# Gate and up products spread over eight PSUM banks, and the transposes of the attention output put on other banks and later, in a two-layer streaming encoder

## The reference, cut to what matters

```python
def ffn_half(x, g, w_gate, w_up, w_down):
    h = rms_norm(x, g)
    a = jax.nn.silu(jnp.einsum('bsd,df->bsf', h, w_gate)) * jnp.einsum('bsd,df->bsf', h, w_up)
    return x + 0.5 * jnp.einsum('bsf,fd->bsd', a, w_down)
...
for l in range(DEPTH):                       # 2 layers
    yp = ffn_half(yp, g_ffn1[l], ...)        # D_MODEL 1024, D_FF 2816
    qa, ka, va, qb, kb, vb = project(rms_norm(yp, g_mix[l]), w_in[l], ...)
    oa = band_attn_prompt(qa, ka, va, ...)   # group A: 8 heads of 64, own chunk of 64 rows and 8 before
    ob = diff_post(diff_attn_prompt(qb, kb, vb, lam), ...)  # group B: 4 heads, softmax 1 - lam * softmax 2
    yp = yp + out_proj(oa, ob, w_out[l])
    yp = ffn_half(yp, g_ffn2[l], ...)
    # the same for ys, the next 64 frames of running streams, against their caches
```

## Time and profile before

| | |
|---|---|
| runs of the kernel before | 8454.6, 8012.99 and 7601.93 us, median 8012.99 |
| profiled execution | 7586.13 us, span 7585.1 us on the slowest core |
| spans of the 8 cores | 7554.7 to 7585.1 us, mean granted clock 0.958 to 0.965 |
| busy: PE, DVE, ACT, POOL | 6630.0, 2912.0, 2651.3, 1403.3 us |
| moved | 1130.56 MB, 149 GB/s over the span |

### The profile page before, as it was taken

The page is one execution under the profiler, slowest core; times in us unless marked ns, Lnnn a source line. Parts: engine busy times, 40 slices in busy tenths (PEclk is TensorE's granted clock), DMA queues, the critical chain, the costliest instruction groups (busy, mean ns, idle before and its releaser), DMA issues.

```text
span 7585.1 us, 114887 instructions; the slowest of 8 cores (7554.7 to 7585.1 us)
## 1 busy us (share of the span) xinstructions
PE 6630.0 (87%) x39776; PEld 3525.2 (46%) x39776; DVE 2912.0 (38%) x5057; ACT 2651.3 (35%) x4204; POOL 1403.3 (19%) x1750
## 2 busy tenths in 40 slices
PE   5777788989899998989898989899999989896777
PEld 2333334454444445454444454544444454555666
DVE  4545534343333343333434343433343433433332
ACT  1412315151524335261414152524333351614343
POOL 1112111202111121212121212121121212122121
PEclk9899999999999999999999999999999999998888
DMA  8699762424233342424242424243343424256666
GB/s 264 216 310 306 224 206 85 146 86 157 97 121 122 115 154 69 147 73 160 97 146 98 158 89 142 95 148 116 109 134 103 148 70 149 77 181 213 208 222 200
DMA packets 452258, 1130.56 MB, mean 149 GB/s; under 512 B 38384, under 2 KB 166128, under 8 KB 451696
## 3 DMA queue, kind: packets, MB, share of 16 engines
q1 hardware_dynamic: 433568, 1059.23, 43.5%
q0 software_dynamic: 18128, 63.97, 2.2%
HBM read 973.12 MB, written 149.95 MB: 148 GB/s over the span
## 4 chain that ended last, share of the span: by engine, by line
PE 61%; DVE 11%; ACT 10%; issue 7%; DMA 5%; POOL 4%; SPq 2%; DVEq 0%; ACTq 0%; POOLq 0%
PE psb L542 14%; PE psb L522 12%; PE psb L518 11%; PE psb L756 5%; POOL tC L533 4%; PE psb L889 3%; PE psb L986 3%; PE psb L1007 3%; DVE tA L528 2%; PE psb L696 2%; ACT tA L531 2%; ACT eT L1065 2%; SPq L270 1%; PE psb L1166 1%; ACT tq L759 1%
## 5 line engine op out<-in xcount | busy, mean ns | idle before, releaser
L533 POOL TENSOR_TENSOR tC<-tA,rstdT 128x512 f32<-128x512 f32 (+1 forms) x792 | 954.4, 1205 | 4198.5 <-ACT tA L531 4081.0
L522 PE MATMUL psb<-hT,wring 128*128 128x512 bf16 (+1 forms) x6336 | 1430.9, 369 | 132.3 <-DVE BIG L536 126.6
L518 PE MATMUL psb<-hT,wring 128*128 128x512 bf16 (+1 forms) x6336 | 1434.5, 369 | 87.2 <-DVE tA L528 78.6
L542 PE MATMUL psb<-BIG,wring 128*128 128x512 bf16 (+1 forms) x6336 | 1322.5, 370 | 43.8 <-DVE wring L412 38.6
L531 ACT ACTIVATE tA<-tA 128x512 f32<-128x512 f32 (+1 forms) x792 | 479.8, 606 | 2218.3 <-DVE tA L528 2217.9
L536 DVE TENSOR_TENSOR BIG<-psb,tC 128x512 bf16<-128x512 f32 (+1 forms) x792 | 524.2, 662 | 1757.8 <-POOL tC L533 1757.8
L522 PEld LDWEIGHTS psb<-hT,wring 128*128 128x128 bf16 x6336 | 588.1, 98 | 895.0 <-issue 355.3
L518 PEld LDWEIGHTS psb<-hT,wring 128*128 128x128 bf16 x6336 | 618.9, 98 | 785.6 <-issue 133.4
L542 PEld LDWEIGHTS psb<-BIG,wring 128*128 128x128 bf16 x6336 | 621.1, 98 | 735.4 <-issue 76.9
L528 DVE TENSOR_TENSOR tA<-psb,rstdT 128x512 f32<-128x512 f32 (+1 forms) x792 | 515.7, 651 | 164.7 <-ACT rstdT L485 164.6
L994 ACT ACTIVATE eT<-psb 128x1024 bf16<-128x1024 f32 (+2 forms) x640 | 532.7, 892 | 106.4 <-PE psb L986 57.5
(11 more groups left out here) (179 smaller groups left out, 6233.0 us busy)
## 6 DMA issues: line engine op xcount, KB each, us to landing
wring<-wsc SPq DMA_DIRECT2D x1280, 512.0 KB, 3.9
wsc<-wring SPq DMA_DIRECT2D x160, 512.0 KB, 9.4
vb<-w_gate SPq DMA_DIRECT2D x66, 512.0 KB, 9.7
vb<-w_up SPq DMA_DIRECT2D x66, 512.0 KB, 10.7
vb<-w_down SPq DMA_DIRECT2D x66, 512.0 KB, 12.3
vb<-cbk SPq DMA_DIRECT2D x64, 512.0 KB, 5.1
vb<-cbv SPq DMA_DIRECT2D x64, 512.0 KB, 4.5
vb<-w_in SPq DMA_DIRECT2D x36, 512.0 KB, 11.6
```

Of the source, the lines that this page charges most:

```text
L518: P.add("pe", lambda kc=kc, bg=bg, wg=wg, fl=fl: nc.tensor.matmul(psb[bg][:, 0:T], wg[:, kc, fl * 128:(fl + 1) * 128], hT[:, kc, 0:T], sta ...
L522: P.add("pe", lambda kc=kc, bu=bu, wu=wu, fl=fl: nc.tensor.matmul(psb[bu][:, 0:T], wu[:, kc, fl * 128:(fl + 1) * 128], hT[:, kc, 0:T], sta ...
L533: P.add("pool", lambda ts=ts: nc.gpsimd.tensor_tensor(out=tC[ts][:, 0:T], in0=tA[ts][:, 0:T], in1=rstdT[:, 0:T], op=ALU.mult), [("t", ts, ...
L542: P.add("pe", lambda: nc.tensor.matmul(psb[ab][:, 0:T], wd[:, fl, dcl * 128:(dcl + 1) * 128], aT[:, fc, 0:T], start=(fc == 0), stop=(fc == ...
```

## The change

Three things are edited. In `ffn` the pair of banks is now `2 * (fc % 4)` and the next, so the pairs go round all eight banks and block fc has the pair of block fc - 4. `rot()` was called 44 times in a pass of `ffn`, a multiple of 4, so its state for the other users is as before. `o_transpose` takes its bank as an argument: in group B's part the transposes of a head come 4 tiles after its last one for i = 0 (2 before) and 6 for i = 1 (4 before), both in bank 4 now; for i = 2 and 3 they stay 6 tiles after it in bank 6. Those of the last head are moved from after unit 4 to after unit 6 of group A, in bank 7. In `a2` the call of `o_transpose(0, hp - 1)` now stands ahead of the norm of u = 3, not behind it.

```diff
             for fl in range(2):
                 fc = 2 * ft + fl
-                bg, bu = rot(), rot()
+                bg = 2 * (fc % 4)
+                bu = bg + 1
...
-        def o_transpose(half, hh):
-            bt = 6
+        def o_transpose(half, hh, bt):
             pv = psb[bt][:, 0:256].bitcast(BF16)
...
-                    deferred.append([idx + min(nk // 2, 6), o_transpose, (1, h)])
+                    lag = 4 if i == 0 else 6
+                    deferred.append([idx + lag, o_transpose, (1, h, 6 if lag <= nk // 2 else 4)])
...
+            if u == 3 and hp > 0:
+                o_transpose(0, hp - 1, 6)
             if u % 2 == 1:
                 ob4 = psb[ob][:, 0:260].rearrange("p (x f) -> p x f", x=4)
...
-            if u == 3 and hp > 0:
-                o_transpose(0, hp - 1)
...
-            if idx == 4:
-                flush(10 ** 9)
-        o_transpose(0, 3)
+            if idx == 6:
+                for d_ in deferred:
+                    d_[1](1, 3, 7)
+                deferred.clear()
+        o_transpose(0, 3, 6)
```

## The result

The changed kernel took 7842.65, 7508.26, 7720.16 and 7487.98 us, median **7614.21 us** (a fifth execution, not in the median, took 7481.87); the kernel before, with one run more than in front, has a median of 7807.46. In part of the executions of either kernel the cores of one die run at a lower granted clock and the time is some per cent longer, and the ratios here leave such executions out while the medians do not. The ratio is **0.9863, 95% interval 0.9817 to 0.9909**; measured again (r1_changed_again) it was 0.9878, 0.9852 to 0.9903. So the change makes the kernel 1.2 to 1.4% faster by these two measurements. The forecast was 7467 us in a range of 7415 to 7545, a ratio of 0.984.

A forecast was written before the change was run, and what follows sets the result against it. PE's work bounds the kernel, with some 955 us of standing; in gate and up the ring DVE, ACT, POOL, DVE sets the pace. 66.4 + 0 + 4.8 + 35 + 13 = 119 us off 7586.1 gives 7467 us, range 7415 to 7545.

The forecast's parts named there:

- the target and its range: Whole kernel: 7467 us, range 7415 to 7545, forecast given 0.62, for an execution like the profiled one.
- the sum: Whole kernel: gains of 66.4, 0, 4.8, 35 and 13 us, 119 us together, taken from 7586.1 us.
- within 2%: Whole kernel: a change too small to be told from no change, about 2%, given 0.77.
- Gate and up, 512 columns: 28 passes after the first group: eight banks move PE forward 11 matmuls, 2.37 us a pass, 66.4 us.
- the first rival: Gate and up products: the whole gap goes, 113 in place of 66.4 us, 7420 us in all; chance 0.12.
- First group: Its four passes: 0 gained, as down products await weight casts on DVE; at most 9.5 us.
- Last group: Its four passes of 256 columns: 11 matmuls of 0.109 us gained in each, 4.8 us.
- Group A: 16 attentions, transposes ahead of the norm: 0.95 us at two boundaries and 0.3 at the end, 35 us.
- Group B, i = 0: Attention, later transposes: a head takes 7.3 us in place of 8.36, 1.1 us gained 12 times, 13 us.
- The clock: The 28 passes: a granted clock of 0.92 would cost 287 us more, 7754 us in all; chance 0.04.
- the rival for a slower kernel: The 28 passes: new waits or denser work lower PE's clock, deciding from 0.965 on, 7754 us; chance 0.04.
- The five terms: Gate and up 66.4 us, first group 0, last group 4.8, group A's attention 35, group B's 13.

The follow-up runs named there:

- r1_changed_again: The changed kernel measured once more, nothing edited, against the kernel before: ratio 0.9878, 0.9852 to 0.9903; median over all its executions 7627.6 us.

## Why the prediction was right or wrong

**The step that failed is the target and its range.** The prediction said that the runs shown "have a median of 8012.99, but their fastest, 7601.93, is what the profiled execution answers to, and the prediction is for an execution of that kind". It thereby put at nothing the time that an execution loses when the cores of one die run at a lower granted clock, and built the range of 7415 to 7545 from costs of the change alone. The runs showed that loss in its place: 7720.16 and 7842.65 us, with the cores of one die at a mean clock of 0.905 and 0.882, beside 7487.98 us with all cores at 0.953 to 0.958. The median over the four executions, 7614.21, is the mean of 7508.26 and 7720.16. The three executions at 7481.87, 7487.98 and 7508.26 us lie inside the range, 15 to 41 us above the 7467. The warning was on record: two of the three runs shown lay 427 and 868 us above the profiled execution, with the same program, and each is more than every term of the sum. What makes a die run at the lower clock in one execution and not in the next is open. The ratio was right: 0.984 forecast, inside the first interval and 0.001 outside the second; so was "within 2%", to which the prediction gave 0.77.

**Gate and up, 512 columns: right, in size and in mechanism.** 66.4 us were forecast, 108.5 - 42.2 = 66.3 came on core 0, from stretches of 77.0 and 76.2 us and a new wait at the fourth down matmul. The 28 waits are 0.45 to 2.37 us and 36.8 us together, where 1.0 or 2.3 and some 46 were forecast: the forecast took 81.57 and 79.48 us for every stretch before, and the means of the 14 of each kind are 81.18 and 79.37. Six banks, the order of the first down matmuls and the opened ring each moved that wait as the mechanism says, and the first rival, the whole gap, is out. By its ratio the edit alone gave 57 us; the difference to 66 is within its interval (35 to 78).

**First group: right.** Its gate and up stretch stood still, 104.30 us, and its four stretches together (441.9 us before, 440.5 after): PE waits for the casts where it waited for the banks. The group as a whole is 14.0 us shorter and its attention stages 14.4, so what attention gained there counted.

**Last group: the term was mis-sized,** 4.8 us forecast, 0.9 found on core 0 (300.8 us for the four passes before, 299.9 after; 296.9 in the second profile). The sum took one wait behind which nothing changes. What the trace shows is a ring of 2.23 us a block against PE's 16 x 0.109 = 1.74, so that PE waits twice, at the second down matmul for block 18 and at the fourth for block 19, and the matmuls behind come slower. The timeline of core 0, and the windows of this down stage before and, behind the line, after:

```profile
7029.21 0.27 PE L543 MATMUL psb<-BIG,wring 128*128 128x256 bf16 x1
7030.57 0.60 PE L543 MATMUL psb<-BIG,wring 128*128 128x256 bf16 x2 [1.09 <-DVE BIG L537]
7032.80 13.03 PE L543 MATMUL psb<-BIG,wring 128*128 128x256 bf16 x101 [1.63 <-DVE BIG L537]
```

```profile
7145.90:7167.80 21.90, 20.14 (x183) 17.40 (x181) 5.60 (x16) 2.89 (x7) 1.41 (x2) 1.00 0.75 248
```

```profile
7029.20:7055.10 25.90, 22.16 (x183) 18.17 (x181) 7.01 (x20) 3.73 (x9) 2.87 (x4) 0.93 0.66 205
```

The 101 matmuls take 13.03 us, where 101 x 0.109 and 0.16 for the last record would be 11.2. So the clock took 1.8 us of a pass whose banks gave 11 x 0.109 = 1.2. It is so in all four passes of the group (0.93 and 0.94 in their down stages, 1.00 before), and in the second profile.

**Group A: right.** On core 0 the transposes now follow each other at 5245.40, 5251.25 and 5257.10, 5.85 us apart where 5.86 was forecast. At the end PE waits twice, 0.68 and 0.35 us, not once for 1.2. In all 39 us of stages on core 0 against 35 forecast.

**Group B, i = 0: right.** A head takes 7.30 us, as forecast; from the timeline of core 0:

```profile
4019.64 0.58 PE L960 MATMUL psb<-identb,hT 128*128 128x128 bf16 x4 [0.75 <-DVE tB L933]
...
4026.94 0.59 PE L960 MATMUL psb<-identb,hT 128*128 128x128 bf16 x4 [0.75 <-DVE tB L933]
```

Against the earlier trace rows the wait is 0.75 us and not 3.68: most of PE's waiting moved to other places of the chain, and the chain itself got 1.06 us shorter. i = 0 gave 13.1 us, 13 forecast.

**The clock: partly right.** It was the rival for a slower kernel and did not decide: behind the new waits of the 28 passes the matmuls keep their 0.215 us. But it took a share. The sum was 119 us, core 0 showed 109 and the ratios 93 to 104, and the mean granted clock of core 0 went from 0.960 to 0.957. The five terms gave 119.5 us on core 0 (66.3, 0, 0.9, 39.2 and 13.1); what is missing lies in stages that the sum left out, 5.6 us in the output products, 3.4 in group B's attention at i = 1 to 3 and 2.8 in the rest of the last group, with 1.9 gained in the projections. The output products, whose order and banks are untouched, show the clock. Two windows of them, of the kernel before and, behind the line, at the same place of the changed one, core 0:

```profile
2107.50:2122.90 15.40, 15.40 (x74) 6.92 (x72) 8.67 (x15) 4.41 (x7) 0.00 (x0) 1.00 0.32 102
```

```profile
2066.80:2083.80 17.00, 17.00 (x73) 7.41 (x73) 8.67 (x15) 4.41 (x7) 0.00 (x0) 0.90 0.29 93
```

Same matmuls, PE busy throughout, 1.6 us more at 0.90. It is so at six of the fourteen such places after the first group, and the other way round at two. The kernel with the attention edits and four banks has the lower clock at ten of the fourteen, the changed kernel at ten, the kernel before at six, so it goes with the attention edits more than with the banks, by one execution each. Which waits tip it is open.

## What to carry to other kernels

When an engine waits for a buffer, look for the loop behind it before adding buffers: here DVE, ACT, POOL and DVE again ran in a closed ring 2% slower than the matrix engine, eight banks moved the wait to the first product that reuses the last bank and gained only what PE does in between, and six banks made the kernel slower than four. Recording one multiplication a block later opened the ring and gave nearly as much again as the whole change (0.9863 to 0.9754); on four banks it gave less (0.9954 to 0.989). And a forecast of a time must hold the spread of the times that are shown, not only the terms of the change.

## What was not expected of the hardware

Waits of the same length left PE's clock alone at some places and halved it at others. With the ring opened on four banks the wait of 2.2 to 2.7 us at the start of a pass of `ffn(l, 1)` is followed by matmuls that start 0.43 us apart for a while in all fourteen passes. In the kernel before the same wait (2.31 us, once 2.60) is followed by matmuls 0.215 us apart in ten of fourteen, and by slower ones in four. In the changed kernel no single wait at the start of the down products, up to 2.37 us (nine matmuls in 2.10 us), is followed by slower ones, in 28 of 28, while two waits of 1.09 and 1.63 us with two matmuls between them are, in four of four of the last group, and so are two of 1.8 to 2.3 and 2.2 to 2.7 us with one matmul between them in the kernel with six banks, in 28 of 28. What decides it is open. Where the clock falls it costs 1.6 to 1.8 us, as much as a good part of the wait itself.
